# Reordering the opening of a two-block transformer kernel: loads in order of need, the context norm behind two products, squares added on GpSimd, a third extra weight slot

## The chip, the cores and the metric

The kernel runs on one core of one Trainium2 chip. Its time is the device time of one launch in microseconds (us), taken as the median over several runs. The core has TensorE (matmuls, PE in the trace), VectorE (DVE), ScalarE (ACT), GpSimd (POOL) and SyncE (SP), which here only issues transfers.

## The reference, cut to what matters

Two blocks on 256 tokens of width 1024, in float32. The opening of the first block is what this change touches:

```
m = silu(cond) @ w + b                       # ada_mod, for c and for c_ctx: shift, scale, gate ...
xn  = rms_norm(h,  norm_mix_g[layer]) * (1 + sc1) + sh1
xcn = rms_norm(hc, norm_mix_g[layer]) * (1 + csc1) + csh1      # the context
y, y_c = even_mixer(xn, xcn, mix_in_w[j], ...)                 # q, fourier features, k, v of x; k, v of the context
h = h + g1 * y
```

Then come the mixer's attention and Fourier part, a gated feed-forward layer, a pooling layer with its own feed-forward layer, and a second block of another kind.

## The kernel before

Activations lie feature by feature: `[128, 8, 256]`, eight groups of 128 features by 256 tokens. Every float32 product is made of three fast ones: an operand x is split in `hi` (ScalarE, L1375 for weights, L1416 for activations) and `lo = x - hi` (VectorE, L1889 and L1921), and TensorE adds hi*hi, hi*lo and lo*hi (L562 to L564). A weight "unit" is 1024 columns, that is one output group; a product of one unit is 24 matmuls.

Weights come through `PLAN`, a fixed list of chunks of `[128, 2048]` (1024 KB). SP issues the loads in this order, each into a slot; before it reuses a slot it waits until the chunk in it is consumed, and everything behind this load waits too. There are four ring slots and, for chunks 0 to 29, two extra ones. Each engine walks the same plan in its own program and keeps count of slots and units with a `Flow` (`take`, `raw`, `used`, `split_to`). A product splits up to three units ahead.

There are two ways in which modulation columns are computed. The first 1024 (the shifts) come from chunks `ada0` on TensorE: `csil` as weights, 512 columns at a time, summed over four chunks into two PSUM banks, copied to a row and transposed. All others come from chunks `adaT0` (two rows of 1024 per partition) on VectorE: a multiply-and-add over a row with the broadcast `silu(c)` in `cB[:, 0]`, about 1.2 us for each. The context needs the columns 8 to 15 as well, with `cB[:, 1]`; these are the chunks adaT 4 to 7, and VectorE runs both products on a row one after the other (L1959, L1961), the second in place.

The order of the opening before:

- SP issues crow (both conditions), adaT 4, ada0 0, adaT 5, ada0 1, adaT 6, ada0 2, and, as slots come free, adaT 7, ada0 3, ctx, mixin 0, adaT 8, and so on. ScalarE issues cols, con0 and xT.
- TensorE takes ada0 0 and 1, the mean square of x as one-column matmuls over the eight groups (`mean_square`, L590, two matmuls for each group, each of them two instructions), ada0 2 and 3, the transposes of the shift, the mean square of the context in the same way, `spread` (L642, the inverse deviation over all partitions), and then the products q0, q1, q2, q3, with the rotation of each q (L708) behind the next product. Then f0 to f3, q4, the context's k, and v.
- VectorE takes the rows of adaT 4 to 7, `scaled`, unit 0's split, `apply("mix0")` (L1915 and L1921, groups of x in turn with ScalarE), the splits of units 1 to 3, and then by turns splits, `turned(n)` (the rotary embedding, L1986 to L1989), `ada(0, 8)` and `ada(0, 9)`, and at last `apply("ctx")`.

For later layers there is another form of the mean square, `mean_square_rest`: GpSimd adds the squares of the groups 0 to 6 one after the other (`sums`, L2600) and TensorE needs only two steps, one for the sum and one for group 7. Likewise `opening` is a form of the first two products of a layer that takes both units together, group by group, as the modulated groups arrive.

## Time and profile before

| what | value |
|---|---|
| runs (3), median | 1209.53 us |
| runs, lowest and highest | 1207.43, 1212.42 us |
| profiled execution, from the first to the last instruction | 1207.4 us |
| own time of the profiled execution, nearest of the runs shown | 1207.43 us |
| TensorE, VectorE, ScalarE, GpSimd busy | 1149.0, 814.4, 589.9, 81.8 us |
| mean granted clock of TensorE | 0.983 |

The profile is of one execution. The times of its instructions are counted from the span's start. A granted clock of 1.00 is 2.4 GHz, 0.50 is 1.2 GHz. TensorE is busy almost throughout, so it is the gaps in its work, and the stretches at the lower clock, that a change of order can alter. The stretch that the change touches lies between 0 and about 102 us, where the first attention scores begin.

### The profile page before, as it was taken

To read this page: it belongs to the slowest core of one execution; us is meant where nothing else is said; L and a number is where in the kernel's file an instruction comes from. 1 tells how busy PE (TensorE), PEld (TensorE's weight loads), DVE (VectorE), ACT (ScalarE), POOL (GpSimd) and SP (SyncE) were. 2 spreads that over 40 slices of the span, in tenths; PEclk is the share of its full clock that TensorE was granted. 3 is DMA by queue.
4 is the path that set the end of the run, shared out by engine and by line. 5 is a ranking of instruction groups with operands and counts; after the bars stand their busy time and mean duration, and the time that the engine had idled before them with its cause. 6 is when DMAs were issued, how large, how long until landed. Compare 5 with 4: busy or idle time off the path is not lost.

```text
span 1207.4 us, 24317 instructions
## 1 busy us (share of the span) xinstructions
PE 1149.0 (95%) x10429; PEld 1092.4 (90%) x10429; DVE 814.4 (67%) x1490; ACT 589.9 (49%) x1084; POOL 81.8 (7%) x100
## 2 busy tenths in 40 slices
PE   5888789999998999999989999999999999999999
PEld 2687689999997999999989888888999999999999
DVE  3783668898886767555674678787664665877543
ACT  2434556454544545454465557653234445655432
POOL 0000110000011000001100111112600001000000
PEclk9789999999999999999998999999999999999999
DMA  9751548889884555751653232232123464855520
GB/s 388 291 207 60 215 170 329 334 340 349 320 328 174 222 222 223 255 187 43 246 175 105 106 105 80 97 105 71 38 72 106 157 211 159 323 198 185 208 84 14
DMA packets 32363, 226.41 MB, mean 188 GB/s; under 512 B 3584, under 2 KB 4736, under 8 KB 5120
## 3 DMA queue, kind: packets, MB, share of 16 engines
q1 hardware_dynamic: 30528, 221.20, 49.1%
q10 hardware_dynamic: 1728, 3.67, 0.8%
q8 instruction: 82, 1.34, 0.4%
q14 instruction: 25, 0.20, 0.1%
HBM read 223.80 MB, written 1.05 MB: 186 GB/s over the span
## 4 chain that ended last, share of the span: by engine, by line
PE 86%; DVE 8%; ACT 4%; DMA 1%; issue 1%; POOL 0%; SPq 0%; DVEq 0%; POOLq 0%
PE bank L562 23%; PE bank L563 22%; PE bank L564 22%; PE bank L1041 2%; PE bank L687 2%; DVE sb_tmp L1915 1%; DVE sb_ring L1930 1%; DVE sb_wlo L1889 1%; PE bank L580 1%; PE bank L1032 1%; PE bank L1063 1%; DMA sb_ring<-in_ada 1%; PE bank L590 1%; PE bank L600 1%; PE bank L1229 1%; PE bank L1247 1%
## 5 line engine op out<-in xcount | busy, mean ns | idle before, releaser
L562 PE MATMUL bank<-sb_xh,sb_whi 128*128 128x256 f32 x1488 | 422.9, 284 | 9.0 <-DVE sb_wlo L1889 6.7
L563 PE MATMUL bank<-sb_xl,sb_whi 128*128 128x256 f32 x1488 | 414.3, 278 | 0.0
L564 PE MATMUL bank<-sb_xh,sb_wlo 128*128 128x256 f32 x1488 | 414.3, 278 | 0.0
L1889 DVE TENSOR_TENSOR sb_wlo<-sb_ring,sb_whi 128x1024 fp32r<-128x1024 f32 (+1 forms) x197 | 239.1, 1220 | 138.5 <-ACT sb_whi L1375 138.1
L562 PEld LDWEIGHTS bank<-sb_xh,sb_whi 128*128 128x128 f32 x1488 | 281.6, 189 | 17.6 <-issue 12.8
L563 PEld LDWEIGHTS bank<-sb_xl,sb_whi 128*128 128x128 f32 x1488 | 282.2, 190 | 0.1
L564 PEld LDWEIGHTS bank<-sb_xh,sb_wlo 128*128 128x128 f32 x1488 | 281.7, 189 | 0.0
L1375 ACT ACTIVATE sb_whi<-sb_ring 128x1024 fp32r<-128x1024 f32 (+1 forms) x197 | 206.7, 1053 | 88.7 <-PE bank L564 81.3
L1889 DVE TENSOR_TENSOR sb_wlo<-sb_more,sb_whi 128x1024 fp32r<-128x1024 f32 x108 | 131.0, 1222 | 64.8 <-ACT sb_whi L1375 64.8
L562 PE MATMUL bank<-sb_hh,sb_whi 128*128 128x256 f32 x608 | 168.4, 277 | 0.0
L564 PE MATMUL bank<-sb_hh,sb_wlo 128*128 128x256 f32 x608 | 167.8, 276 | 0.0
L563 PE MATMUL bank<-sb_hl,sb_whi 128*128 128x256 f32 x608 | 167.8, 276 | 0.0
L1375 ACT ACTIVATE sb_whi<-sb_more 128x1024 fp32r<-128x1024 f32 x108 | 114.0, 1057 | 66.2 <-PE bank L564 56.1
L563 PEld LDWEIGHTS bank<-sb_hl,sb_whi 128*128 128x128 f32 x608 | 114.2, 188 | 0.0
L562 PEld LDWEIGHTS bank<-sb_hh,sb_whi 128*128 128x128 f32 x608 | 114.1, 188 | 0.0
L564 PEld LDWEIGHTS bank<-sb_hh,sb_wlo 128*128 128x128 f32 x608 | 114.1, 188 | 0.0
L1930 DVE CUSTOM_DVE_ANT_0 sb_ring<-sb_ring,sb_cB,sb_col 128x1024 f32<-128x1024 f32 x46 | 58.0, 1299 | 0.0
L1536 ACT ACTIVATE sb_tmp<-bank 128x256 f32<-128x256 f32 x44 | 16.9, 384 | 66.2 <-PE bank L564 66.2
L1397 ACT ACTIVATE sb_sq<-sb_h 128x256 f32<-128x256 f32 x48 | 19.2, 415 | 58.9 <-DVE sb_h L1944 54.2
L2600 POOL TENSOR_TENSOR sb_sq<-sb_sq 128x256 f32<-128x256 f32 x24 | 19.2, 801 | 367.2 <-ACT sb_sq L1397 366.3
L1930 DVE CUSTOM_DVE_ANT_0 sb_more<-sb_more,sb_cB,sb_col 128x1024 f32<-128x1024 f32 x34 | 42.7, 1292 | 0.0
L1667 ACT ACTIVATE sb_ss<-sb_ss,sb_st 128x128 f32<-128x128 f32 x64 | 28.1, 442 | 7.2 <-DVE sb_st L2303 7.2
(378 smaller groups left out, 1845.6 us busy)
## 6 DMA issues: line engine op xcount, KB each, us to landing
sb_more<-in_w SPq DMA_DIRECT2D x34, 1024.0 KB, 6.7
sb_ring<-in_w SPq DMA_DIRECT2D x32, 1024.0 KB, 6.0
sb_ring<-in_adaT SPq DMA_DIRECT2D x26, 1024.0 KB, 7.6
sb_ring<-in_f SPq DMA_DIRECT2D x22, 1024.0 KB, 5.0
sb_more<-in_adaT SPq DMA_DIRECT2D x18, 1024.0 KB, 9.5
sb_ring<-in_gn SPq DMA_DIRECT2D x8, 1024.0 KB, 4.9
sb_ring<-in_gd SPq DMA_DIRECT2D x8, 1024.0 KB, 4.9
sb_ring<-in_up SPq DMA_DIRECT2D x8, 1024.0 KB, 5.9
```

The source lines that it names most:

```text
L562: te.matmul(out, wh, rh, start=start, stop=False, skip_group_check=skip)
L563: te.matmul(out, wh, rl, start=False, stop=False, skip_group_check=skip)
L564: return te.matmul(out, wl, rh, start=False, stop=stop, skip_group_check=skip)
L687: end = te.matmul(ps_of(("row", e))[0:2, :], csil[:, k, :], w[:, o:o + 512], start=k == 0, stop=k == KT - 1)
L1041: end = te.matmul(ps[:, k * 128:(k + 1) * 128], ss[:, i % 3, u, k * 128:(k + 1) * 128], dg2[:, i % 2, 2 * u + (k > 0), :], start=True, sto ...
L1375: sc.activation(hi, x, ACT.Copy).then_inc(*hi_done.up(n))
L1397: sc.activation(sq[:, k, :], src[:, k, :], ACT.Square).then_inc(*act.up(("sq", norm, k)))
L1536: sc.activation(temp(("silu", layer, j), (dve, ("hid", layer, j))), ps_of(("up", layer, j))[:, 0:T], ACT.Silu).then_inc(*act.up(("silu", l ...
L1667: sc.activation(p, p, ACT.Exp, bias=x[:, 1, u, t:t + 1], scale=slope((2 * aa + u) * 4 + r), accum_out=x[:, 2, u, t:t + 1]).then_inc(*act.u ...
L1889: ve.tensor_tensor(lo, x, hi.bitcast(F32), ALU.subtract).then_inc(*lo_dve.up(n))
L1930: ve.tensor_tensor_reduce(out=x, in0=x, in1=cB[:, 0, :], scale=1.0, scalar=C(f"ab{layer}", jj, jj + 1), op0=ALU.mult, op1=ALU.add, accum_o ...
L2600: gp.tensor_tensor(sq[:, 0, :], sq[:, 0, :], sq[:, k, :], ALU.add).then_inc(*pool.up(("sum", norm, k)))
```

## The change

- The plan begins with ada0 0, ada0 1, adaT 4, ada0 2, adaT 5, ada0 3, mixin 0, adaT 6, adaT 7, adaT 8, mixin 1. crow is loaded in two halves, the row of c behind ada0 0, that of the context behind ada0 2. xT and con0 go from ScalarE's queue to SP's, in front of mixin 0; ctx comes in front of mixin 1, con1 in front of mixin 2.
- Chunks 0 to 29 have three extra slots.
- Both norms of the opening use `mean_square_rest` and `sums`: six additions on GpSimd for each, and 8 instead of 32 one-column instructions on TensorE.
- TensorE makes q0 and q1 with `opening`, straight behind the spread. The context's mean square comes behind these two products and in front of q2; its squares on ScalarE come behind the copies of units 2 and 3. The rotations of q0 and q1 come behind q2.
- VectorE first takes the rows with c of adaT 4 and 5, then their rows with the context's condition, then the splits of units 0 and 1, then the rows with c of adaT 6 and 7. The context rows of these two come behind `apply("mix0")` and the splits of units 2 and 3, then `ada(0, 8)`, and only then the turns of q0 and q1.

```diff
     for i in range(4):
-        add("adaT0", 1, split=False, first=4 + i)
         add("ada0", 1, split=False, first=i)
-    for i in range(5):
-        add("mixin", 1, first=i)
-        if i < 4:
-            add("adaT0", 1, split=False, first=8 + i)
+        if i in (1, 2):
+            add("adaT0", 1, split=False, first=3 + i)
+    add("mixin", 1)
+    add("adaT0", 2, split=False, first=6)
+    for i in range(4):
+        add("adaT0", 1, split=False, first=8 + i)
+        add("mixin", 1, first=1 + i)
...
-    extra = [(0, len(p), 2)]
+    extra = [(0, len(p), 3)]
...
@@ tensor_program
-                idle(2)
+                idle(2 * (norm not in ("mix0", "ctx")))
...
-                if i == 1:
-                    P.wait_ge(s_con0, 16)
-                    for k in range(KT):
-                        mean_square("mix0", k)
+                if i in (1, 2):
+                    F.used(F.raw("adaT0"))
+            P.wait_ge(s_con0, 16)
+            mean_square_rest("mix0")
             ps = take(RA, "shift", (dve, "shift"))
...
-            for k in range(KT):
-                mean_square("ctx", k)
+            F.split_to(1)
             spread("mix0")
+            first = [F.take("mixin", 0)[0] for _ in range(2)]
+            late = [F.raw("adaT0") for _ in range(2)]
...
-            F.split_to(0)
-            F.split_to(2)
-            for n in range(4):
+            q01 = [take(RG, ("q", n), (act, ("qraw", n)))[:, 0:T] for n in range(2)]
+            opening("mixin", "mix0", [(ps, True) for ps in q01], [("q", n) for n in range(2)], first)
+            F.early(2)
+            F.used(F.raw("adaT0"))
+            mean_square_rest("ctx")
+            for n in (2, 3):
                 u, _ = F.take("mixin")
                 ps = take(RG, ("q", n), (act, ("qraw", n)))
                 product(u, xh, xl, "mix0", ps[:, 0:T]).then_inc(*pe.up(("q", n), ("unit", u)))
-                if n > 0:
-                    rotate(n - 1)
-                if n % 2:
-                    F.used(F.raw("adaT0"))
-                if n == 1:
-                    spread("ctx")
+                for m in ((0, 1), (2,))[n - 2]:
+                    rotate(m)
+                F.used(late[n - 2])
+            F.used(F.raw("adaT0"))
+            spread("ctx")
             rotate(3)
...
@@ scalar_program
-                    A.wait_ge(s_con0, 16)
-                    sc.activation(warm[:, :], ones[:, 0:1], ACT.Sqrt).then_inc(*act.up())
+                    sc.activation(warm[:, :], C("eps"), ACT.Sqrt).then_inc(*act.up())
...
+            deviation("mix0")
+            split(F.split_to(1))
+            for _ in range(2):
+                F.done(F.take("mixin", 0)[0])
+            late = [F.raw("adaT0") for _ in range(2)]
+            upper("mix0", mods[:, 0, 0:8], xh)
+            split(F.early(2))
             for k in range(KT):
                 square("ctx", k, ctxr, (s_ctx, 16), ("ms", "mix0"))
-            split(F.split_to(0))
-            upper("mix0", mods[:, 0, 0:8], xh)
-            split(F.split_to(2))
-            deviation("ctx")
...
+            turned_raw(0)
+            turned_raw(1)
+            deviation("ctx")
...
@@ vector_program
+            for c in rows:
                 for u in range(2):
+                    row_ctx(c, u)
+            split(F.split_to(1))
...
+            row_c(late[0], 0)
+            row_c(late[0], 1)
+            row_c(late[1], 0)
+            inverse_deviation("mix0")
             V.wait_ge(*pe.at("shift"))
...
+            row_c(late[1], 1)
             V.wait_ge(*dve.at("ada", 0, 15))
             scaled(0, C("nm", 0, 8), mods[:, 0, 8:16])
...
             apply("mix0", h, scl[:, 0, :], mods[:, 0, 0:8], xh, xl)
-            split(F.split_to(2))
-            inverse_deviation("ctx")
+            split(F.early(2))
+            for c in late:
+                for u in range(2):
+                    row_ctx(c, u)
...
+            ada(0, 8)
+            V.wait_ge(*dve.at("adac", 15))
+            scaled(1, C("nm", 0, 8), cmod[:, 8:16])
+            turned(0)
+            turned(1)
+            inverse_deviation("ctx")
...
@@ gpsimd_program
+            sums("mix0")
+            sums("ctx")
...
@@ sync_program
-            sp.dma_start(cB[:, :, :], a["crow"]).then_inc(s_c, 16)
             for c in range(len(PLAN)):
-                if c == 8:
+                if c == 1:
+                    sp.dma_start(cB[:, 0, :], a["crow"][:, 0, :]).then_inc(s_c, 16)
+                if c == 4:
+                    sp.dma_start(cB[:, 1, :], a["crow"][:, 1, :]).then_inc(s_cc, 16)
+                if c == 6:
+                    sp.dma_start(h[:, :, :], a["xT"]).then_inc(s_x, 16)
+                    sp.dma_start(con[0][:, :], a["con0"]).then_inc(s_con0, 16)
+                if c == 10:
                     sp.dma_start(ctxr[:, :, :], a["ctxT"]).then_inc(s_ctx, 16)
-                if c == 13:
+                if c == 12:
                     sp.dma_start(con[1][:, :], a["con1"]).then_inc(s_con1, 16)
                 load(c)
```

`row_c(c, u)` is one row product with `cB[:, 0]` whose full-length output goes to `junk`; `row_ctx(c, u)` is the one with `cB[:, 1]`, in place. A slot of adaT 4 to 7 is free when its `row_ctx` are done.

## Rows read from the trace of the kernel before

**Rows 1.** The page: span, engines, TensorE's busy tenths in 40 slices, the chain's lines.
```profile
span 1207.4 us, 24317 instructions
...
PE 1149.0 (95%) x10429; PEld 1092.4 (90%) x10429; DVE 814.4 (67%) x1490; ACT 589.9 (49%) x1084; POOL 81.8 (7%) x100
...
PE   5888789999998999999989999999999999999999
...
PE bank L562 23%; PE bank L563 22%; PE bank L564 22%; PE bank L1041 2%; PE bank L687 2%; DVE sb_tmp L1915 1%; DVE sb_ring L1930 1%; DVE sb_wlo L1889 1%; PE bank L580 1%; PE bank L1032 1%; PE bank L1063 1%; DMA sb_ring<-in_ada 1%; PE bank L590 1%; PE bank L600 1%; PE bank L1229 1%; PE bank L1247 1%
```
**Rows 2.** The chain in order of time, 0 to 48 us: start, length, what.
```profile
1.63 12.34 DMA sb_ring<-in_ada
14.02 9.85 PE bank L687 x16
23.87 4.44 PE bank L590 x32
...
39.61 6.34 PE bank L590 x32
...
47.05 0.49 DVE sb_tmp L1915
```
**Rows 3.** The same chain, 58 to 102 us.
```profile
58.74 0.40 PE bank L708 x2
59.27 0.42 DVE sb_tmp L1986
...
60.48 1.20 DVE sb_ring L1930
...
62.89 1.14 DVE sb_wlo L1889
...
70.99 0.49 DVE sb_tmp L1915
...
77.40 0.96 ACT sb_whi L1375
...
79.75 0.55 PE bank L562
...
101.53 1.09 PE bank L759 x8
```
**Rows 4.** Windows: length, busy of five engines, clock, DMA share, GB/s.
```profile
2.00:2.50 0.50, 0.00 (x0) 0.00 (x0) 0.00 (x0) 0.36 (x1) 0.00 (x0) 1.00 0.31 66
15.00:20.00 5.00, 5.00 (x8) 0.73 (x6) 3.19 (x5) 2.19 (x8) 0.00 (x0) 1.00 1.01 421
```
**Rows 5.** Timeline of ScalarE, opening: start, length, instruction, idle before.
```profile
6.64 0.22 ACT L1424 ACTIVATE sb_csil<-sb_col 128x16 f32<-128x16 f32 x1 [3.22 <-DMA sb_col<-in_cols]
...
14.63 2.56 ACT L1397 ACTIVATE sb_sq<-sb_h 128x256 f32<-128x256 f32 x8 [4.45 <-DMA sb_h<-in_xT]
...
41.35 1.04 ACT L1375 ACTIVATE sb_whi<-sb_ring 128x1024 fp32r<-128x1024 f32 x1
```
**Rows 6.** Timeline of GpSimd where it adds squares, and later.
```profile
325.48 1.26 POOL L2600 TENSOR_TENSOR sb_sq<-sb_sq 128x256 f32<-128x256 f32 x1 [145.57 <-ACT sb_sq L1397]
...
386.15 5.07 POOL L2600 TENSOR_TENSOR sb_sq<-sb_sq 128x256 f32<-128x256 f32 x6 [21.46 <-ACT sb_sq L1397]
...
848.70 1.77 POOL L2649 TENSOR_TENSOR sb_sq<-sb_R,sb_con 128x256 f32<-128x256 f32 x1 [1.34 <-DVE sb_R L2458]
```
**Rows 7.** Timeline of VectorE at the same places.
```profile
324.87 1.27 DVE L1930 CUSTOM_DVE_ANT_0 sb_ring<-sb_ring,sb_cB,sb_col 128x1024 f32<-128x1024 f32 x1
...
326.07 1.75 DVE L1930 CUSTOM_DVE_ANT_0 sb_ring<-sb_ring,sb_cB,sb_col 128x1024 f32<-128x1024 f32 x1
...
851.25 0.90 DVE L2476 TENSOR_TENSOR sb_qk<-sb_con,sb_sq 128x256 f32<-128x256 f32 x1
```
**Rows 8.** Windows of 1 us around changes of the clock.
```profile
53.00:54.00 1.00, 1.00 (x6) 0.93 (x5) 0.80 (x2) 1.00 (x2) 0.00 (x0) 0.57 0.00 0
...
77.00:78.00 1.00, 0.00 (x0) 0.00 (x0) 0.74 (x2) 1.00 (x2) 0.00 (x0) 0.88 0.00 0
```

More of the change, by code:

```diff
@@ L581, in column_sums @@
                 return end
-            def mean_square(norm, k):
-                if k == 0:
-                    for t in range(2):
-                        take(RA, ("ms", norm, t), (act, ("sd", norm)))
-                P.wait_ge(*act.at("sq", norm, k))
-                for t in range(2):
-                    end = te.matmul(ps_of(("ms", norm, t))[:, t:t + 1], sq[:, k, t * 128:(t + 1) * 128], ones[:, 0:1], start=k == 0, stop=k == KT - 1)
-                if k == KT - 1:
-                    end.then_inc(*pe.up(("ms", norm)))
             idles = iter(range(100))
@@ L649, in settle, with opening @@
                 te.matmul(ps[:, 0:64], x[:, 2, 0:128], x[:, 0, 0:64], start=True, stop=True)
-            def opening(name, norm, outs, steps):
-                us = [F.take(name)[0] for _ in outs]
+            def opening(name, norm, outs, steps, us=None):
+                us = us or [F.take(name)[0] for _ in outs]
                 for u in us:
@@ L1401, in deviation @@
                 A.wait_ge(*pe.at("ms", norm))
-                if norm in ("mix0", "ctx", "mix2"):
-                    for t in range(2):
-                        sc.activation(d[:, t:t + 1], ps_of(("ms", norm, t))[:, t:t + 1], ACT.Sqrt, bias=C("eps"), scale=1.0 / D).then_inc(*act.up(*[("sd", norm)] * t))
-                else:
-                    sc.activation(d, ps_of(("ms", norm, 0))[:, 0:2], ACT.Sqrt, bias=C("eps"), scale=1.0 / D).then_inc(*act.up(("sd", norm)))
+                sc.activation(d, ps_of(("ms", norm, 0))[:, 0:2], ACT.Sqrt, bias=C("eps"), scale=1.0 / D).then_inc(*act.up(("sd", norm)))
             def upper(norm, shift, hi, free=None):
@@ L1425, in scalar_program @@
             A.wait_ge(s_c, 16)
-            sc.activation(cB[:, :, :], cB[:, :, :], ACT.Silu).then_inc(*act.up("cB"))
+            sc.activation(cB[:, 0, :], cB[:, 0, :], ACT.Silu).then_inc(*act.up("cB"))
+            A.wait_ge(s_cc, 16)
+            sc.activation(cB[:, 1, :], cB[:, 1, :], ACT.Silu).then_inc(*act.up("cBc"))
             for i in range(4):
-                F.used(F.raw("adaT0"))
                 F.used(F.raw("ada0"))
-                if i == 1:
-                    for k in range(KT):
-                        square("mix0", k, h, (s_x, 16), None)
-                    deviation("mix0")
+                if i in (1, 2):
+                    F.used(F.raw("adaT0"))
+            for k in range(KT):
+                square("mix0", k, h, (s_x, 16), None)
             for e in range(2):
@@ new lines, in row_ctx @@
+            def row_ctx(c, u):
+                jj = 2 * PLAN[c][1] + u
+                x = chunk(c)[:, u * 1024:(u + 1) * 1024]
+                V.wait_ge(*act.at("cBc"))
+                V.wait_ge(*dve.at("ada", 0, jj))
+                ve.tensor_tensor_reduce(out=x, in0=x, in1=cB[:, 1, :], scale=1.0, scalar=C("ab0", jj, jj + 1), op0=ALU.mult, op1=ALU.add,
+                                        accum_out=cmod[:, jj:jj + 1]).then_inc(*dve.up(("adac", jj)))
+            rows = []
+            for i in range(4):
+                F.used(F.raw("ada0"))
+                if i in (1, 2):
+                    c = F.raw("adaT0")
+                    rows.append(c)
+                    for u in range(2):
+                        row_c(c, u)
+                    F.used(c)
@@ L1967, in vector_program @@
+            for c in rows:
+                for u in range(2):
+                    row_ctx(c, u)
+            split(F.split_to(1))
+            for _ in range(2):
+                F.done(F.take("mixin", 0)[0])
+            late = [F.raw("adaT0") for _ in range(2)]
+            row_c(late[0], 0)
+            row_c(late[0], 1)
+            row_c(late[1], 0)
+            inverse_deviation("mix0")
             V.wait_ge(*pe.at("shift"))
@@ L1989, in turned @@
                 ve.tensor_tensor(dst, raw, r3, ALU.add).then_inc(*dve.up(("q", n)))
-            for n in range(4):
+            ada(0, 8)
[4 more added lines that the diff above has]
+            inverse_deviation("ctx")
+            for n in (2, 3):
                 weights("mixin")
-                if n > 0:
-                    turned(n - 1)
-                if n % 2:
-                    ada(0, 8 + n // 2)
+                if n == 3:
+                    turned(2)
+                F.used(late[n - 2])
+            ada(0, 9)
             turned(3)
```

40 lines of the change are left out of this document (15 added, 25 removed).

## Prediction

> **What bounds the kernel now.** I read the page first: TensorE is busy for 95% of the span [rows 1], so only the places where it has no products can give time back, and the busy tenths put the largest at the very start [rows 1]. The change touches that start, so next came the chain of waits in order of time. It runs without a gap from the first transfer on [rows 2]: 12.3 us until the first ada0 chunk lands (it stands third in SP's queue), ada0 products, 32 one-column mean-square matmuls (4.4 us), the rest of ada0, 32 more for the context (6.3 us), the spread (1.1), and at 47.05 VectorE begins to modulate x ("apply mix0"). Then VectorE sets the pace: it turns q0 from 59.27, and after turns, weight splits and two pairs of rows begins to modulate the context at 70.99; ScalarE and VectorE split unit 7 behind that, and TensorE, which has been idle 4.5 us for this unit, starts f3 at 79.75 [rows 3]. From there it has f3, q4, kc and four v products in one piece until the first scores at 101.53. Thus **the number that decides is when "apply ctx" starts on VectorE**: 70.99 before. All that follows (30.5 us to the scores, then a ping-pong that the change leaves alone) shifts with it.
>
> **Transfers after the change.** The stream starts between 2.0 and 2.5 us and runs at 420 GB/s [rows 4], 2.5 us for a chunk of 1024 KB. Bytes by this rate plus 0.7 us until the semaphore give back the old landings within 0.5 us: ahead of the old ada0 chunk 0 stood crow, one adaT chunk, cols, con0 and nearly all of xT, and it landed at 13.97 [rows 2]. In the new order this gives: ada0 chunk 0 at 6.3, row c 7.5, ada0 1 10.0, adaT 4 12.5, ada0 2 15.0, context row 16.3, adaT 5 18.8, ada0 3 21.3, **xT 23.8** (it landed at 14.6 before, as the squares show [rows 5]), con0 24.3, mixin 0 26.8, adaT 6 29.3, adaT 7 31.8, then ctx 36.8, mixin 1 39.3, con1 44.4, mixin 2 46.9. The chunks that must wait for a slot are issued ahead of the moment at which the stream reaches them (the latest, behind the context rows of adaT 4 and 5, at about 24 and 27), so the third extra slot keeps the stream full. SP now issues eleven transfers at once instead of seven, some 0.45 us each (the fourth chunk's issue lies in the first 3 us), done by 6 us: hidden behind the stream.
>
> **TensorE's opening.** csil is ready at 6.9 as before [rows 5]. The first two chunks of ada0 took 9.85 us together, part slow and part fast [rows 2]; chunks 0 to 2 run from 6.9 in some 14 us, and chunk 3, landed at 21.3, takes at most 5: 26.3. This isn't the path. xT is: squares at 0.32 us each [rows 5], two ready at 24.4, then six additions on GpSimd.
>
> **The price of an addition.** With VectorE on light work six took 5.07 us, 0.845 each. But one that fell into an ada row took 1.26, and the next row 1.75 instead of 1.27 [rows 6, 7]; a multiplication of GpSimd beside a weight split took 1.77 [rows 6], and a VectorE product beside GpSimd 0.90 [rows 7] instead of some 0.42 [rows 3]. So each waits for the other's end: while VectorE goes from one row to the next, one addition fits per row, and the pair costs 1.20 + 0.48 = 1.68 us. The Trainium skill (SBUF — State Buffer, Who interferes with whom) says as much: a VectorE instruction with two SBUF inputs and a GpSimd instruction that reads SBUF exclude each other for the whole instruction. The trace agrees with 1.26 and 1.75. By this rule the sum is that of rival A below (+6.5 us), by the six additions in 5.07 us that of B (+2.0).
>
> **The x norm.** VectorE is in its context rows of adaT 4 and 5 from 21.2 to 26.5. The first addition waits until 24.8, the second until 26.5, the other four run alone: done at 30.5. Eight one-column matmuls at the slow clock (6.34 us for 32 [rows 2]) 1.6: 32.1. Deviation on ScalarE 0.3, and only then its first weight copy (0.95 to 1.04 [rows 3, 5]): 33.4. VectorE, idle since 26.5, stands with its splits of units 0 and 1 in front of the late rows, whose data are there by 31.8: two splits 2.3, three rows of 1.2, reciprocal and shifts 0.3, fourth row 1.2, scale 0.2: **apply mix0 at 41.0, 6.0 us earlier**. The spread (1.1) hides behind the fourth row.
>
> **The first two products.** xh 0 is there at 42.0. The old first product began at 48.7 and the clock rose in the 54th us [rows 8]. So 22 of the 48 matmuls at 0.21, 26 at 0.12: 50.0, where q1 ended before 58.7 [rows 3]. The modulation takes 6.4 us until ScalarE is free (70.99 to 77.40 for the context, which has the same form [rows 3]) and 6.9 until VectorE is, so it ends at 47.9, hidden beneath them.
>
> **The context norm, now in front of q2.** TensorE goes to the context mean square before q2. ScalarE ends the upper halves at 47.4, copies units 2 and 3 (49.3), then squares: the second is there at 50.05. VectorE splits unit 3 until 50.6 and goes straight into four context rows and adaT 8, six rows in a piece. So the first addition is done at 51.2 and five more at 1.68 us: **59.6**. TensorE idles for 9.6 us, falls to the slow clock (it fell within the old 4.5 us gap, in the 78th us [rows 8]), does the mean square (1.6, 61.2) and q2 slowly, 24 x 0.21 = 5.1: 66.3. The rotation of q0 now stands behind q2, 0.5 to 0.7 us until VectorE can start on it [rows 3]: 67.0. VectorE has been idle since 61; the 6 us that it waits here are the new wait. It still has two turns (2.3), a reciprocal (0.1), three splits (3.4), a turn (1.1), adaT 9 (2.4) and a turn (1.1), 10.4 in all (a turn is 1.2 or less, a row 1.20, a split 1.14 in the chain [rows 3]): **apply ctx at 77.5 against 70.99, 6.5 us later**. Units 4 and 5 are copied from 61.5, unit 6 has landed before 60. f0 to f2 end by 79, so f3 still starts behind unit 7 and at the slow clock, and the 30.5 us from apply ctx to the scores stay.
>
> **Edits at nothing.** One square root of two columns for two of one: 0.2 us, within the 0.3 above. The square's table warmed from eps: no wait. The slots of the attention stage: the only transfer among the chain's lines on the page is the ada0 chunk [rows 1], so earlier loads have nothing to give there; from w13 on each chunk waits for the same predecessor.
>
> **The sum.** -6.0 at apply mix0, then +12.5 between it and apply ctx (36.5 against 23.9): +6.5 us on a span of 1207.4. The runs' median is 2.1 us above that span, the fastest run equals it. So 1213.9 as span and **1216.0** as median. Bounds of the disputed price: an addition costs 0.845 (its row with VectorE light) to 1.68; I take 1.68, since rows of the same form show it.
>
> **Rivals.**
> A, the forecast: additions and rows alternate, +6.5, 1216. Speaks against: the pattern is shown for one addition between two rows, not for six. Own range +3.5 to +10.
> B, no lasting exclusion (GpSimd gets through at 0.845): sums done at 55.1, apply ctx 73.0, +2.0: 1211.5. The 1.26 and 1.75 speak against it.
> C, the other side, not slower: q2's delay is not passed on, because the mean square is ready when q1 ends. Then VectorE alone sets apply ctx: free of rows at 57.8, + 10.4 = 68.3, 2.7 us earlier: 1206.8. It needs the sums by 50.7 or so, or a q2 that starts before 54.5 with the fast clock; ScalarE's order (squares behind units 2 and 3) speaks against it.
> D, dearer: VectorE, going from row to row, lets GpSimd in only after its last one. It would be through at 50.6 + 6 x 1.20 = 57.8, six additions at 0.845 end at 62.9, 3.3 later than in A: +9.8, 1219.3. A stream that doesn't take eleven waiting transfers would cost about as much. Against the first speaks that the one addition did get in between two rows [rows 6, 7].
>
> **How the numbers follow.** A 0.60, B 0.18, C 0.10, D 0.12. 0.5% is 6 us, about what a measurement of this kernel can tell from no change, and A lies just beyond this bound, so a little over half of it is slower. Slower: 0.32 of A's 0.60 and 0.11 of D's 0.12, 0.43. Faster: the part of C in which the gain of 6 us is carried through, 0.05. Same 0.52. Range 1208 (B with its spread, a part of C) to 1221 (A with its spread, most of D).
>
> **What the profile after would show.** First ada0 product near 7; xT landing near 24; apply mix0 near 41; GpSimd's additions for x done near 30.5, for the context stretched to about 1.7 each while rows of VectorE show 1.75; a hole of 8 to 11 us on TensorE after q1, at half clock; q2 slow; VectorE idle before it turns q0; apply ctx near 77.5; the scores near 108. It goes wrong if the additions of the context end near 55 (B), if q2 doesn't wait for them, or if xT lands elsewhere than at 23.8, since the first half hangs on it one for one.

## The result and the profile after

The changed kernel takes 1220.55 us (median of 4 runs, 1218.65 to 1221.74) where the kernel before takes 1209.49 (4 runs on the same chip, 1207.43 to 1212.42): ratio 1.0094, 95% interval 1.0064 to 1.0123. It is slower, by 11 us. The forecast was 1216.0 with 1208 to 1221.

The page of the changed kernel. The last of the lines shown is the clock that TensorE was granted, in tenths of full speed:

```profile
span 1219.6 us, 24242 instructions
...
PE 1147.6 (94%) x10382; PEld 1093.4 (90%) x10382; DVE 818.0 (67%) x1490; ACT 590.1 (48%) x1083; POOL 96.2 (8%) x112
...
PE   5379889999998999999999999999999999999999
...
PEclk9679989999999999999999999999999999999999
```

TensorE is busy as long as before (1147.6 against 1149.0 us [rows 1]), but the span is 12.2 us longer. GpSimd has 14.4 us more, for twelve additions. The second and third slices of TensorE's line read 3 and 7 where before they read 8 and 8 [rows 1]: that is the opening.

The chain of waits of the changed kernel, opening up to "apply mix0" (start, length, what), which answers to [rows 2]:

```profile
4.86 19.73 DMA sb_h<-in_xT
24.61 1.96 ACT sb_sq L1389 x6
26.57 1.52 POOL sb_sq L2621
...
30.82 0.73 POOL sb_sq L2621
...
34.16 2.36 DVE sb_wlo L1883 x2
36.52 1.20 DVE sb_junk L1950
...
42.23 0.49 DVE sb_tmp L1909
```

The bound has moved from TensorE's ada0 products to xT, then GpSimd, then VectorE. "Apply mix0" starts at 42.23, 4.8 us before the old 47.05 [rows 2]. Experiment e6 below shows how little this difference is worth: there the unchanged opening of the old kernel reached the same mark at 40.64.

The same chain from the context norm to the scores, which answers to [rows 3]:

```profile
51.32 1.26 POOL sb_sq L2621
...
59.37 1.53 POOL sb_sq L2621
60.94 1.01 PE bank L599 x4
...
67.92 0.42 DVE sb_tmp L2001
...
78.44 0.49 DVE sb_tmp L1909
...
87.20 0.55 PE bank L564
...
108.47 1.09 PE bank L752 x8
```

Two timelines show why. First VectorE, then GpSimd, in the same stretch (start, length, instruction, and in brackets the idle time before it with what ended it):

```profile
51.90 1.75 DVE L1958 CUSTOM_DVE_ANT_0 sb_ring<-sb_ring,sb_cB,sb_col 128x1024 f32<-128x1024 f32 x1
...
53.58 1.73 DVE L1958 CUSTOM_DVE_ANT_0 sb_ring<-sb_ring,sb_cB,sb_col 128x1024 f32<-128x1024 f32 x1
...
60.24 1.73 DVE L1924 CUSTOM_DVE_ANT_0 sb_ring<-sb_ring,sb_cB,sb_col 128x1024 f32<-128x1024 f32 x1
...
67.92 0.42 DVE L2001 TENSOR_TENSOR sb_tmp<-bank,sb_con 128x256 f32<-128x256 f32 x1 [5.87 <-PE bank L699]
```

```profile
51.32 9.56 POOL L2621 TENSOR_TENSOR sb_sq<-sb_sq 128x256 f32<-128x256 f32 x6 [19.78 <-ACT sb_sq L1389]
```

Rows that take 1.27 us with GpSimd idle [rows 7] take 1.73 to 1.75, one addition goes with each row, and their starts lie 1.66 to 1.68 us apart. TensorE waits for the last addition, VectorE then waits 5.87 us for TensorE.

The windows of the changed kernel in that hole and behind it, and then in attention (length, busy time of PE, PEld, DVE, ACT and POOL, granted clock, DMA share, GB/s):

```profile
52.00:61.00 9.00, 0.11 (x3) 0.06 (x1) 9.00 (x11) 1.62 (x6) 8.17 (x6) 0.74 0.51 151
61.00:67.00 6.00, 6.00 (x30) 6.00 (x31) 1.06 (x3) 2.15 (x3) 0.00 (x0) 0.54 0.90 351
112.00:114.00 2.00, 0.44 (x2) 0.45 (x3) 0.79 (x3) 1.68 (x7) 0.38 (x1) 1.00 0.00 0
114.00:116.00 2.00, 2.00 (x8) 1.59 (x7) 0.91 (x5) 1.02 (x4) 0.23 (x1) 0.58 0.00 0
116.00:118.00 2.00, 2.00 (x6) 1.30 (x5) 0.66 (x3) 1.51 (x5) 0.06 (x1) 0.57 0.00 0
168.00:170.00 2.00, 2.00 (x11) 2.00 (x11) 1.49 (x2) 0.50 (x2) 0.00 (x0) 0.50 0.00 0
```

TensorE has 0.11 us of work between 52 and 61, and does the context's mean square and q2 at 0.54, near the level of 1.2 GHz. The last windows show something that the forecast did not have. In attention the clock falls again while TensorE is busy. In the profile of before it stays at 1.00 there:

```profile
107.00:109.00 2.00, 2.00 (x11) 1.77 (x10) 0.97 (x5) 0.96 (x4) 0.30 (x1) 1.00 0.00 0
109.00:111.00 2.00, 2.00 (x16) 1.29 (x15) 0.73 (x4) 1.74 (x7) 0.00 (x0) 1.00 0.00 0
```

So the 12.2 us of span come in two parts. At the first scores the changed kernel is 6.94 us late (108.47 against 101.53 [rows 3]), and the rest is lost behind them. (The span of before belongs to the shortest of its four runs, so 12.2 is a little more than the 11 us between the medians.) The table below follows this for every kernel run. "Scaled" is VectorE's first instruction that scales scores, 1.25 us behind the first score product; "apply ffn0" is the first modulation of the feed-forward layer.

| profile | apply mix0 | apply ctx | scaled | scaled to apply ffn0 | span |
|---|---|---|---|---|---|
| before | 47.05 | 70.99 | 102.78 | 81.99 | 1207.4 |
| before, second profile (e9) | 47.58 | 71.52 | 103.36 | 81.28 | 1207.8 |
| after | 42.23 | 78.44 | 109.72 | 85.89 | 1219.6 |
| after, second profile (e10) | 42.58 | 78.73 | 109.97 | 85.27 | 1222.7 |
| e1 rows behind turns | 42.34 | 82.24 | 113.17 | 83.79 | 1220.6 |
| e2 norm behind q3 | 42.41 | 73.16 | 104.36 | 84.63 | 1214.3 |
| e3 ctx sums on TensorE | 42.24 | 71.01 | 102.36 | 84.02 | 1209.2 |
| e4 two extra slots | 42.33 | 77.35 | 111.89 | 83.99 | 1219.9 |
| e5 hole filled | 42.26 | 77.51 | 109.08 | 80.77 | 1213.8 |
| e6 before, delayed | 40.64 | 64.66 | 102.31 | 85.49 | 1213.5 |
| e7 late rows first | 38.76 | 74.78 | 105.72 | 83.80 | 1212.7 |
| e8 both on TensorE | 38.20 | 69.29 | 100.43 | 80.72 | 1204.5 |
| e11 GpSimd undone | 39.45 | 68.98 | 100.55 | 80.74 | 1204.3 |
| e12 e8 with fillers | 45.26 | 75.11 | 104.95 | 83.54 | 1214.0 |

The stretch from "scaled" to "apply ffn0" as one window each, before and after (columns as in the windows above, the granted clock third from the end):

```profile
102.78:184.77 81.99, 69.45 (x574) 61.09 (x574) 51.09 (x116) 44.32 (x103) 9.34 (x14) 1.00 0.39 144
```

```profile
109.72:195.61 85.89, 75.02 (x574) 66.32 (x574) 51.26 (x116) 44.52 (x103) 9.32 (x14) 0.92 0.35 125
```

TensorE runs the same 574 instructions in both and is busy 5.6 us longer. Its waits in this stretch don't grow: the longest is 3.12 us before and 3.13 after. In all fourteen profiles the stretch takes 80.7 to 82.0 us where its mean granted clock is 1.00 (five of them) and 83.5 to 85.9 where it is 0.92 to 0.96 (nine). So the second part is TensorE's clock, and not another wait.

### The profile page after: what moved, and what is told of

Same layout as the page of the kernel before. It is cut to its first block, busy times and chain, and to the rows that moved or that the text cites. A ratio compares the mean times of both kernels' runs of the same rounds, so it can differ in the third digit from the quotient of the medians.

```text
span 1219.6 us, 24242 instructions
## 1 busy us (share of the span) xinstructions
PE 1147.6 (94%) x10382; PEld 1093.4 (90%) x10382; DVE 818.0 (67%) x1490; ACT 590.1 (48%) x1083; POOL 96.2 (8%) x112
## 4 chain that ended last, share of the span: by engine, by line
PE 82%; DVE 9%; ACT 4%; DMA 2%; POOL 1%; issue 1%; SPq 0%; POOLq 0%; DVEq 0%; ACTq 0%
PE bank L564 23%; PE bank L565 22%; PE bank L566 22%; PE bank L1034 2%; DMA sb_h<-in_xT 2%; DVE sb_wlo L1883 2%; POOL sb_sq L2621 1%; DVE sb_tmp L1909 1%; PE bank L582 1%; PE bank L1056 1%; ACT sb_whi L1368 1%; PE bank L1025 1%; DVE sb_more L1924 1%; PE bank L591 1%; PE bank L1222 1%
## 5 line engine op out<-in xcount | busy, mean ns | idle before, releaser
L564 PE MATMUL bank<-sb_xh,sb_whi 128*128 128x256 f32 (+1 forms) x1472 | 417.2, 283 | 8.1 <-DVE sb_wlo L1883 7.7
L565 PE MATMUL bank<-sb_xl,sb_whi 128*128 128x256 f32 (+1 forms) x1472 | 410.0, 279 | 0.0
L566 PE MATMUL bank<-sb_xh,sb_wlo 128*128 128x256 f32 (+1 forms) x1472 | 409.9, 278 | 0.0
L1883 DVE TENSOR_TENSOR sb_wlo<-sb_ring,sb_whi 128x1024 fp32r<-128x1024 f32 (+1 forms) x197 | 239.4, 1221 | 142.6 <-ACT sb_whi L1368 142.2
L564 PEld LDWEIGHTS bank<-sb_xh,sb_whi 128*128 128x128 f32 (+1 forms) x1472 | 278.7, 189 | 15.8 <-issue 12.7
L565 PEld LDWEIGHTS bank<-sb_xl,sb_whi 128*128 128x128 f32 (+1 forms) x1472 | 278.8, 189 | 0.1
L566 PEld LDWEIGHTS bank<-sb_xh,sb_wlo 128*128 128x128 f32 (+1 forms) x1472 | 278.5, 189 | 0.0
L1883 DVE TENSOR_TENSOR sb_wlo<-sb_more,sb_whi 128x1024 fp32r<-128x1024 f32 x108 | 130.6, 1223 | 65.4 <-ACT sb_whi L1368 65.4
L2621 POOL TENSOR_TENSOR sb_sq<-sb_sq 128x256 f32<-128x256 f32 x36 | 33.5, 929 | 417.2 <-ACT sb_sq L1389 415.1
L1924 DVE CUSTOM_DVE_ANT_0 sb_ring<-sb_ring,sb_cB,sb_col 128x1024 f32<-128x1024 f32 x40 | 51.5, 1326 | 0.0
L1924 DVE CUSTOM_DVE_ANT_0 sb_more<-sb_more,sb_cB,sb_col 128x1024 f32<-128x1024 f32 x40 | 50.2, 1292 | 0.0
L2655 POOL TENSOR_TENSOR sb_dg<-sb_con,sb_st 128x512 f32<-128x512 f32 x16 | 17.6, 1097 | 202.1 <-DVE sb_st L2332 202.1
## 6 DMA issues: line engine op xcount, KB each, us to landing
sb_more<-in_w SPq DMA_DIRECT2D x34, 1024.0 KB, 6.2
sb_ring<-in_w SPq DMA_DIRECT2D x32, 1024.0 KB, 6.2
sb_ring<-in_adaT SPq DMA_DIRECT2D x23, 1024.0 KB, 7.6
sb_ring<-in_f SPq DMA_DIRECT2D x22, 1024.0 KB, 4.9
sb_more<-in_adaT SPq DMA_DIRECT2D x21, 1024.0 KB, 8.7
sb_ring<-in_gn SPq DMA_DIRECT2D x8, 1024.0 KB, 4.9
sb_ring<-in_gd SPq DMA_DIRECT2D x8, 1024.0 KB, 4.9
sb_ring<-in_up SPq DMA_DIRECT2D x8, 1024.0 KB, 5.9
```

The lines of the kernel that those rows point to most:

```text
L564: te.matmul(out, wh, rh, start=start, stop=False, skip_group_check=skip)
L565: te.matmul(out, wh, rl, start=False, stop=False, skip_group_check=skip)
L566: return te.matmul(out, wl, rh, start=False, stop=stop, skip_group_check=skip)
L1883: ve.tensor_tensor(lo, x, hi.bitcast(F32), ALU.subtract).then_inc(*lo_dve.up(n))
L1924: ve.tensor_tensor_reduce(out=x, in0=x, in1=cB[:, 0, :], scale=1.0, scalar=C(f"ab{layer}", jj, jj + 1), op0=ALU.mult, op1=ALU.add, accum_o ...
L2621: gp.tensor_tensor(sq[:, 0, :], sq[:, 0, :], sq[:, k, :], ALU.add).then_inc(*pool.up(("sum", norm, k)))
```

## The experiments

All are edits of the changed kernel if not said otherwise. Ratios are to the kernel before on the same chip.

**e1, the context rows behind the turns of q0 and q1.** This takes all of VectorE's rows away from beside GpSimd's additions.

```diff
             split(F.early(2))
-            for c in late: ... row_ctx(c, u)
 ...
-            ada(0, 8)
-            scaled(1, C("nm", 0, 8), cmod[:, 8:16])
             turned(0)
             turned(1)
             inverse_deviation("ctx")
+            for c in late: ... row_ctx(c, u)
+            ada(0, 8)
+            scaled(1, C("nm", 0, 8), cmod[:, 8:16])
```

> The changed kernel with VectorE's four late context rows and the two rows of adaT 8 moved from in front of the turns of q0 and q1 to behind them. VectorE then stands idle beside the context's additions. Theory (exclusion): the six additions take 5.5 to 6 us instead of 9.6 (51.3 to 60.9), TensorE's hole behind q1 shrinks by 4 us, q2 starts near 58.8 instead of 62.8; but the 7.2 us of rows now lie behind q2's turn, so apply ctx starts near 81.7 (78.4 in the changed kernel) and the time is 3 us above the changed kernel's 1220.6. Rival (the additions are slow on GpSimd by themselves, or wait for ScalarE's squares): the additions still take over 9 us and q2 starts at 62.8 as before; the time is then 7 us above.

Measured: 1222.89 us, ratio 1.0117 (1.0090 to 1.0144). GpSimd's timeline, then two lines of VectorE's:

```profile
51.44 5.58 POOL L2621 TENSOR_TENSOR sb_sq<-sb_sq 128x256 f32<-128x256 f32 x6 [20.42 <-ACT sb_sq L1389]
```

```profile
64.41 0.42 DVE L1998 TENSOR_TENSOR sb_tmp<-bank,sb_con 128x256 f32<-128x256 f32 x1 [12.31 <-issue]
...
66.74 1.27 DVE L1958 CUSTOM_DVE_ANT_0 sb_ring<-sb_ring,sb_cB,sb_col 128x1024 f32<-128x1024 f32 x1
```

The same six additions take 5.58 us where they took 9.56, and the rows 1.27 where they took 1.73. VectorE stood idle meanwhile, 12.31 us until it could turn q0. So the stretching is mutual exclusion of the two engines, not slow additions, and the rival is out. The rows are now in VectorE's way behind the turns, so apply ctx is still later (82.24).

**e2, the context norm behind the fourth product.** TensorE no longer waits for GpSimd ahead of q2. ScalarE's deviation of the context moves behind q3 with it (these lines stand elsewhere in the file and are left out here).

```diff
-            mean_square_rest("ctx")
             for n in (2, 3): ... product, rotate(m)
             F.used(F.raw("adaT0"))
+            mean_square_rest("ctx")
             spread("ctx")
```

> The changed kernel with the context's mean square on TensorE behind q3 instead of in front of q2 (ScalarE's deviation goes with it); GpSimd still adds. Theory (the place of the wait decides, and exclusion lengthens it): q2 follows q1 at 52 at the fast clock, VectorE is the one that sets the pace: it is through with its rows, stretched to 1.7 us each, at 61.9 and starts apply ctx 10.5 us later, at 72.4 (78.4 changed, 71.0 before); the scores start 6 us earlier than in the changed kernel, 1214 to 1215. Rival (the hole is harmless because VectorE is the bound anyway): apply ctx stays at 78, 1220.

Measured: 1213.82 us, ratio 1.0034 (1.0012 to 1.0055). The additions still take 9.64 us beside the rows, but q2 begins at 51.3 and apply ctx comes at 73.16, 5.3 us earlier than in the changed kernel. The rival (the hole is harmless) is out.

**e3, the context's squares summed on TensorE.** 32 one-column products at the place of the change, no addition for the context.

```diff
-            mean_square_rest("ctx")
+            mean_square_all("ctx")   # for k in range(KT): two matmuls 128x1 on sq[:, k]
 ...
-            sums("ctx")
```

> The changed kernel with the context's squares summed on TensorE again (32 one-column instructions over the eight groups, at the place of the two steps); GpSimd has no additions beside VectorE's rows. Theory (exclusion): rows take 1.20 us again, VectorE is through with them at 59.1 instead of 61.9; TensorE's mean square ends near 58.3 instead of 62.8, apply ctx at 74.0, 4.5 us earlier than in the changed kernel: 1216. Rival (GpSimd relieves TensorE, the exclusion costs little): 32 instructions at the slow clock cost as much as the additions, apply ctx at 78 or later, 1220 to 1222.

Measured: 1210.54 us, ratio 1.0012 (0.9996 to 1.0029). The products on TensorE's timeline:

```profile
51.86 3.71 PE L613 MATMUL bank<-sb_con,sb_sq 128*128 128x1 f32 x32
```

They ran in 3.71 us; no hole preceded them. Apply ctx at 71.01 is 7.4 us earlier than in the changed kernel and where it was before the change. The theory had the direction right and the size too small: it expected 74.0 and 1216 us.

**e4, two extra slots as before the change.**

```diff
-    extra = [(0, len(p), 3)]
+    extra = [(0, len(p), 2)]
```

> The changed kernel with two extra slots instead of three. Theory: the stream itself stays full up to 40 us, so apply mix0 stays at 42.2; but mixin 3 (units 6 and 7) then waits for the slot of adaT 7 and unit 6 is split only behind apply ctx, so f2 waits as well as f3: 2 to 3 us slower than the changed kernel, 1223. Rival (the slot does nothing): 1220.5.

Measured: 1221.64 us, ratio 1.0110 (1.0079 to 1.0141). Apply ctx came 1.1 us earlier, since one weight split moved behind it, and the scaled scores 2.2 us later (111.89), since that split was then missing. The stretch behind the scores was 1.9 us shorter in this profile than in that of the changed kernel, so the spans came out alike (1219.9 and 1219.6). In the total the slot can't be told from no slot; the expected 1223 did not come.

**e5, the hole filled.**

```diff
+            idle(20)
             mean_square_rest("ctx")
```

> Edit: 20 products of TensorE into a spare bank (a 128x256 product took 0.43 us at the full clock in the trace of before, so some 8.6 us) fill the hole of 51.9 to 60.9 in the changed kernel, ahead of the context's mean squares; nothing waits for them. Theory H (the hole costs the clock locally): the products of q2 behind it go at the level of 2.4 GHz, 24 products in 2.8 us and not in 4.6, and the mean squares and the spread in some 0.7 us less; the apply of the context comes at 76.0 and not at 78.4, and the time is 1218. Theory K (the hole is also what makes the clock fall later, between 114 and 174): in that stretch too the granted clock is 1.00 throughout as it was before the change, the stretch from the scores to the apply of ffn0 takes 82.0 us as before and not 85.9, and the time is 1214. Rival: DVE is the bound behind the hole, q2 early does not help; the apply stays within 0.5 us of 78.4 and the time at 1220.

Measured: 1218.84 us, ratio 1.0073 (1.0050 to 1.0097). TensorE's timeline:

```profile
50.83 8.36 PE L591 MATMUL bank<-sb_con 128*128 128x256 f32 x38
60.98 0.61 PE L599 MATMUL bank<-sb_con,sb_sq 128*128 128x1 f32 x4 [1.79 <-POOL sb_sq L2622]
...
63.04 0.28 PE L564 MATMUL bank<-sb_xh,sb_whi 128*128 128x256 f32 x1
...
64.10 0.41 PE L564 MATMUL bank<-sb_xh,sb_whi 128*128 128x256 f32 x1
```

The line of fillers leaves out the first two of their forty instructions; all forty took 8.88 us, from 50.32 to 59.20. The first half of the mean square took 0.61 us where it took 1.01, but the clock fell within q2 all the same (a product 0.28 at 63.04, 0.41 at 64.10), and apply ctx gained 0.9 us, not 2.4. In this profile the clock stays at 1.00 from 114 to 170, and the stretch behind the scaled scores took 80.77. Its eight runs range from 1214.97 to 1222.93, those of the changed kernel beside e10 from 1217.68 to 1224.63: theory K fits this profile, which is of one of the shortest executions (1215.63 us), and the median moved too little for it.

**e6, the kernel before, with fillers ahead of the scores.**

```diff
             c_dft = F.raw("dft")
+            idle(15)
             w = chunk(c_dft)
```

> Edit: in the kernel BEFORE the change, 15 products of TensorE into spare banks (0.43 us each) stand ahead of the scores; nothing else is changed, so that attention and all behind it come 6.4 us later, with no hole on TensorE. Theory P (attention that comes at another time or with another history loses clock by itself): from the scores to the apply of ffn0 takes 84 to 86 us and not 82.0, the granted clock falls below 1.00 there, and the time is 1208 + 6.4 + 3 = 1217.5. Rival Q (a late attention costs only its lateness, and what fell in the changed kernel has to do with what the change does): 82.0 us as before, the clock 1.00 from 98 to 166 us and later, the time 1214.8.

Measured: 1217.09 us, ratio 1.0065 (1.0043 to 1.0087). The fillers took 6.69 us, and the stretch from the scaled scores to apply ffn0 took 85.49, as theory P said. The total rose by 8.5 us, with an interval of 5.2 to 10.5 that holds both P and Q. The profile isn't a test of lateness: the scaled scores came at 102.31, no later than in before, because the opening had been faster. The opening is the more interesting part, since the edit can't reach it. The window of 26 to 34 us, in before, in e9 and in e6:

```profile
26.00:34.00 8.00, 8.00 (x22) 3.15 (x22) 5.21 (x10) 0.41 (x2) 0.00 (x0) 0.57 1.01 419
```

```profile
26.00:34.00 8.00, 8.00 (x26) 3.60 (x27) 4.68 (x8) 0.41 (x2) 0.00 (x0) 0.57 1.01 420
```

```profile
26.00:34.00 8.00, 7.75 (x24) 1.98 (x23) 6.73 (x12) 0.63 (x3) 0.00 (x0) 1.00 1.01 422
```

The same instructions on the same data, and the clock is 0.57 in two profiles and 1.00 in one. Apply mix0 came at 40.64, against 47.05 and 47.58. The first ada0 product stands at 14.01 in e6 and at 14.02 in before, and the first difference that I find behind it is again one of TensorE's pace: its ada0 products, 0.86 us each at first, go to 0.43 at 18.2 us in e6 and only at 19.8 in before, so that the first two chunks took 9.12 us and not 9.85. In these early windows the clock reads 1.00 all the same, so the pace, and not that figure, shows this step.

This bears on the change itself. 40.64 is 1.6 us ahead of the changed kernel's 42.23, so the gain of the new order at apply mix0 is there against the two profiles with the slow stretch and not against this one.

**e7, the late rows of c ahead of the splits of units 0 and 1.**

```diff
-            split(F.split_to(1))
+            new = F.split_to(1)
-            row_c(late[0], 0) ... row_c(late[1], 0)
+            for c in late: ... row_c(c, u)
+            split(new)
```

> Edit: in the changed kernel the four late rows of c stand on DVE ahead of the splits of the weights' units 0 and 1 (which GpSimd's additions of x now lie beside), not behind them. Theory M (DVE's queue sets the apply of mix0, and rows beside GpSimd's additions cost 1.7 us and not 1.3): the rows go at 26 to 33 with 1.7 us each, the deviation is not delayed by more than 0.5, the splits follow, and the apply of mix0 comes at 39.0 and not at 42.2; the sums of ctx, its apply and the end follow by what TensorE's order lets through, 2.5 us: apply of the context 76.0, time 1218. Rival (the chunks land too late or the splits' lateness delays q0): the apply of mix0 is earlier than 42.2 by less than 1.5, or it is, and q0 and q1 are not; the time 1220.5.

Measured: 1214.65 us, ratio 1.0038 (1.0020 to 1.0055). VectorE, and GpSimd's additions for x:

```profile
29.95 1.69 DVE L1950 CUSTOM_DVE_ANT_0 sb_junk<-sb_ring,sb_cB,sb_col 128x1024 f32<-128x1024 f32 x1 [2.57 <-DMA sb_ring<-in_adaT]
31.69 1.62 DVE L1950 CUSTOM_DVE_ANT_0 sb_junk<-sb_ring,sb_cB,sb_col 128x1024 f32<-128x1024 f32 x1
33.46 1.28 DVE L1950 CUSTOM_DVE_ANT_0 sb_junk<-sb_ring,sb_cB,sb_col 128x1024 f32<-128x1024 f32 x1
```

```profile
25.30 6.93 POOL L2621 TENSOR_TENSOR sb_sq<-sb_sq 128x256 f32<-128x256 f32 x6 [24.85 <-ACT sb_sq L1389]
```

Two rows are long (1.69, 1.62), the third is not, because GpSimd had finished. Apply mix0 gains 3.5 us and apply ctx 3.7, a little more than theory M said, and the total is 3.4 us below its 1218.

**e8, both mean squares on TensorE, the context norm behind q3, late rows first.**

```diff
-            mean_square_rest("mix0")
+            mean_square_all("mix0")
 ...
             rotate(3)
+            mean_square_all("ctx")       # instead of mean_square_rest ahead of q2
             for j in range(4): ... product f_j
+                if j == 0: spread("ctx")
 ...
+            late rows of c ahead of split(new), as in e7
-            sums("mix0")
-            sums("ctx")
```

> Edit: in the changed kernel both mean squares of the opening are made by one-column products on TensorE (32 each, 3.7 us at the full clock) and GpSimd adds nothing there; the context's norm, its spread and deviation stand behind the fourth product of q and the first of f; the four late rows of c stand ahead of the splits. Theory R (the loss is GpSimd's additions and the place of the context's norm, and the order of need with its early rows is a gain by itself): apply of mix0 38.0, apply of the context 65.5 to 67 (DVE's own queue sets it: no row beside GpSimd), scores 96 to 97, which is 5 to 6 us earlier than before; with 2 to 3 us more in attention, as the other runs had, the time is 1205. Rival S (DVE or the transfers bound the opening in any order): scores not earlier than 100, time 1208 to 1210.

Measured: 1207.88 us, ratio 0.9989 (0.9972 to 1.0006). Apply mix0 at 38.20 was as expected, but apply ctx came only at 69.29, and the scores at 99.2 instead of 96 to 97: VectorE waited 3.63 us for the spread, and ahead of that TensorE did the context's mean square in 6.43 us and f0 at the slow clock.

**e9 and e10, the two kernels unchanged, once more.**

> Edit: none, the kernel before the change once more, for a second profile of it. The run with a delay ahead of the scores had an opening that the delay can't reach, yet its apply of mix0 came at 40.6 and not at 47.1, with the granted clock at 1.00 from 14 to 38 us, where the first profile of before had 0.57 to 0.58 from 26 to 34. Theory V (TensorE's clock in the opening and in attention falls differently from one execution to the next, so that a stage's time in one profile is uncertain by several us, though the total's median is not): this profile differs from the first by more than 2 us in the apply of mix0 or in the stretch from the scores to the apply of ffn0 (82.0), and the total is 1208 to 1209 with single executions from 1205 to 1214. Rival (one schedule, one clock): apply of mix0 at 47.0 and the stretch at 82.0, each within 0.3.

> Edit: none, the changed kernel once more, for a second profile and more times. Theory V (the dips between 114 and 174 in the first profile are one draw of many): the stretch from the scores to the apply of ffn0 comes out between 82 and 86.5 and differs from the first profile's 85.9 by more than 1; apply of mix0 42.2, apply of the context 78.4 both within 0.3 (their waits are not TensorE's), the total 1219 to 1221 with single executions from 1215 to 1223. Rival (the dips belong to the changed schedule): 85.9 again, within 0.5.

Measured: before 1208.86 us (ratio to itself 1.0004, 0.9987 to 1.0022), after 1218.07 us (7 runs, 1217.68 to 1224.63; ratio 1.0078, 1.0050 to 1.0105). The total of the changed kernel is below the 1219 to 1221 expected. The marks and the stretch of the table came back within 0.25 to 0.71 us in both kernels: a little wider than the rival had put, and far from the 2 and 1 us of theory V. In the changed kernel the attention stage lost its clock at the same places. The second profile, which is of the longest of the seven executions, has 3.1 us more span; it lost 3.5 behind apply ffn0. Two windows of e10:

```profile
114.00:118.00 4.00, 4.00 (x12) 3.16 (x11) 1.71 (x8) 2.37 (x8) 0.49 (x1) 0.57 0.00 0
166.00:172.00 6.00, 5.62 (x26) 5.62 (x27) 3.74 (x5) 2.73 (x4) 0.00 (x0) 0.50 0.09 36
```

Theory V, as put, is refuted for these two pairs, though e6 shows the other clock in an unchanged stretch.

**e11, GpSimd's additions undone, all else of the change kept.**

```diff
-            mean_square_rest("mix0")
+            mean_square_all("mix0")
 ...
-            mean_square_rest("ctx")
+            mean_square_all("ctx")
 ...
-            sums("mix0")
-            sums("ctx")
```

> Edit: in the changed kernel GpSimd adds no squares, neither of x nor of ctx; the mean squares are 32 one-column products each on TensorE, at the places in TensorE's order that the change gave them. All else of the change (order of need, one more weight slot, the context's place behind q1) stays. Theory G (GpSimd's additions are what the change loses by): apply of mix0 41.0 to 42.2, apply of the context 70 to 71 as in the run with the context's sums on TensorE, scores 101 to 102, time 1209, no more than 0.2% from before; the order of need then gains about nothing. Rival O (the order loses by itself as well): 1213 or more. Rival N (the order is a gain that GpSimd hid): 1205 or less.

Measured: 1208.09 us, ratio 0.9993 (0.9974 to 1.0011). Theory G: rivals O and N are out. VectorE's timeline:

```profile
31.39 2.36 DVE L1893 TENSOR_TENSOR sb_wlo<-sb_more,sb_whi 128x1024 fp32r<-128x1024 f32 x2 [4.79 <-ACT sb_whi L1378]
...
39.45 0.87 DVE L1919 SCALAR_TENSOR_TENSOR sb_tmp<-sb_h,sb_scl,bank 128x256 f32<-128x256 f32 x2
...
68.98 0.88 DVE L1919 SCALAR_TENSOR_TENSOR sb_tmp<-sb_ctxr,sb_scl,bank 128x256 f32<-128x256 f32 x2
```

The splits start at 31.39 and not at 34.16, apply mix0 comes 2.8 us earlier and apply ctx 9.5 us earlier than in the changed kernel, both somewhat earlier than the theory had said.

**e12, e8 with fillers in its holes.**

```diff
+            idle(12)
             spread("mix0")
+            idle(5)
 ...
+            idle(6)   # ahead of the third rotation
+            idle(6)   # ahead of the fourth product of f
```

> Edit: the kernel with both mean squares on TensorE, the context's norm behind the fourth product of q and the late rows first (which took 1207.9), and in it 29 products of TensorE into spare banks (0.43 us each at the full clock) in its four holes: 12 ahead of the spread of mix0, 5 behind it, 6 ahead of the third rotation, 6 ahead of the fourth product of f. Theory W (its apply of the context was 3.6 us late because TensorE did the context's mean squares in 6.4 us and the first product of f at the level of 1.2 GHz): the mean squares take 3.7, the product 2.8, the apply of the context comes at 65.7 and not at 69.3, and the time is 1204. Rival (the products in the holes end too late and push work, or the clock falls anyhow): the apply at 69 or later, the time at 1207 or above.

Measured: 1215.54 us, ratio 1.0050 (1.0032 to 1.0067). TensorE's timeline:

```profile
29.85 2.08 PE L591 MATMUL bank<-sb_con 128*128 128x256 f32 x4
37.70 7.08 PE L591 MATMUL bank<-sb_con 128*128 128x256 f32 x20 [5.77 <-DVE sb_cmod L2002]
44.62 0.61 PE L643 MATMUL bank<-sb_con,sb_dev 128*128 128x128 f32 x4
...
66.55 3.63 PE L613 MATMUL bank<-sb_con,sb_sq 128*128 128x1 f32 x32
```

My fillers were badly placed: one of them had to wait for the PSUM bank that holds the shift until VectorE had read it, and the others then stood ahead of the spread, which came 9 us late. Behind them the mean square took 3.63 us as theory W said, but f0 was slow all the same (0.41 us a product), and from apply mix0 to apply ctx only 1.2 us were saved (29.85 against 31.09). It says nothing on whether fillers that don't wait would pay.

## Why the prediction was right, and what it lacked

The direction and the mechanism were right up to the scores, and the time lay in the range. The median was 4.6 us above the 1216.0, and in the repetition (1218.07) 2.1. That the range held the first median is partly luck: it lies 0.45 us inside the upper end, 11.1 us above before where rival A's own spread ended at +10, and what filled the difference is neither A's spread nor D, but a loss behind the scores that the sum did not have. The chances leaned the other way too: "same" had 0.52 and "slower" 0.43.

| step | predicted | measured |
|---|---|---|
| xT lands | 23.8 | 24.6 |
| additions for x done | 30.5 | 31.5 (25.41 + 6.12) |
| apply mix0 | 41.0 | 42.23 |
| additions for the context done | 59.6 | 60.9 (51.32 + 9.56) |
| VectorE turns q0 | 67.0 | 67.92 |
| apply ctx | 77.5 | 78.44 |
| f3 starts | 86.3, that is 79.75 + 6.5 | 87.20 |
| first scores | near 108 | 108.47 |

- **The transfers.** The sum by bytes and rate put xT 0.8 us too early, and this error goes through the whole first half. The -6.0 us at apply mix0 (measured -4.8) is also a difference to one profile of before: by e6, another execution of that same opening has no such gain to give.
- **The price of an addition**, 1.68 us beside a row, was taken from one single case in the old trace. Measured: six rows with starts 1.66 to 1.68 apart. e1 shows the cause by its removal. By the Trainium skill (SBUF — State Buffer, Who interferes with whom) the loser waits for the whole instruction; the trace agrees, in both directions: rows of 1.73 instead of 1.28, additions of 1.53 instead of 0.73. The two don't add up in full, though: a row alone advances VectorE by 1.21 us (e1), an addition alone GpSimd by 0.86 (28.23 to 30.82 above, three steps), and a pair by 1.67 and not by 2.07. Rivals B and D are out.
- **The hole and the delay of q2** (rival C's point) came as put: 0.11 us of work in 52 to 61, slow q2, VectorE idle for 5.87 us. e2 and e3 each take this wait away in a way of their own and bring apply ctx back by 5.3 and 7.4 us.
- **Apply mix0 to apply ctx** was to grow to 36.5 us and measured 36.21.
- **What failed is "all that follows ... shifts with it".** It holds until the scores (31.28 us from apply ctx to the scaled scores, 31.79 before). From there to apply ffn0 the changed kernel took 85.89 and 85.27 us in its two profiles, before 81.99 and 81.28: 3.9 to 4.0 us more, at windows of 0.50 to 0.58 that the profiles of before don't have. Behind apply ffn0 the first profile lost a further 1.4 us (1024.0 against 1022.6), the second of after still more. The sum had no term for this.

What made the clock fall in attention stays open. By the windows above it is TensorE's clock and no wait. It is not the lateness of the scores by itself: e5 was as late as the changed kernel (109.08) and took 80.77. Nor is it GpSimd's additions alone: e3, with the context on TensorE and scores as early as before, took 84.02. Nor the order of need, which e8 and e11 keep with 80.72 and 80.74. In e6, the old kernel with fillers ahead of the scores, it took 85.49, with the scaled scores at 102.31 as in before. The fourteen profiles' values fall into two groups, 80.7 to 82.0 and 83.5 to 85.9. Each profile is one execution, and only two kernels were profiled twice, so I can't say what chooses the group.

Part by part, then: GpSimd's additions are what the change lost by, as e11 gives back all of it (0.9993, where the changed kernel measured beside it had 1.0078), and e2 shows that the place of the wait was a good part of their price. That the order of need gains anything isn't shown: without the additions the scaled scores come 2.2 us earlier (100.55 against 102.78), but the old opening in e6 would have had them near 95.6 (an estimate, 102.31 less the fillers' 6.69), and the total shows nothing. The third slot shows nothing in the total. No version tried beats the kernel before measurably; e3, e8 and e11 can't be told from it.

## What to carry to other kernels

GpSimd isn't a free helper for a VectorE that is running two-input instructions: price the pair (here 1.67 us for a row of 1.21 and an addition of 0.86) and not the addition alone, and look at who waits for the last one. A wait put ahead of work that doesn't need it costs that work too; the norm's place behind q3 repaired more than half of the loss without touching the additions. When a forecast ends in "the rest shifts", give that rest a margin for TensorE's clock, here 4 to 5 us of 1210. And before a gain is read off one profile of the old kernel, take a second and a third: its marks can move by more than the gain.

## What the runs showed of the hardware that I had not expected

- The same unchanged opening ran with a granted clock of 0.57 in two profiles and 1.00 in a third (26 to 34 us); "apply mix0" came 6.4 us earlier there. Single executions of the kernel before lie between 1203.60 and 1214.37 us, and those with a lower mean clock are the longer ones: 1204.84 at 0.987, 1208.57 at 0.984, 1214.37 at 0.977.
- 32 one-column products ran in 3.71 us where TensorE had been busy before them (e3) and in 6.43 where, one rotation earlier, it had waited 2.70 us (e8). In e3 the clock then fell within the next product, at 56.3 us, although TensorE had been busy without a break since 44.
- Keeping TensorE busy for 8.88 us with fillers (e5) did not keep the clock up: it fell 4.1 us behind their end, 1.79 of these idle, in the middle of q2.
